# An expert's rows turned by matmuls with its 0/1 matrix, in place of a copy in memory, fetches and transposes

## The reference

```
logits = x @ w_router + b_router              # x: 288 x 1024, 32 experts
top_logit, top_e = top_k(logits, 4)
gate = softmax(top_logit)
for each expert e, over the rows that chose it:
    g, u = split(rows @ w_gu[e] + b_gu[e])     # 1024 -> 2 x 1024
    g = min(g, 7); u = clip(u, -7, 7)
    y = ((u + 1) * g * sigmoid(1.702 * g)) @ w_down[e] + b_down[e]
x = x + ga2 * (sum over a token's 4 experts of gate * y)
```

## Time and profile before

| what | value |
|---|---|
| median of three runs | 1684.99 us |
| profiled execution, own time | 1689.25 us |
| its span, first to last instruction | 1687.6 us |
| TensorE matmuls, busy | 1378.4 us, 82% |
| TensorE weight loads, busy | 724.2 us, 43% |
| VectorE, ScalarE, GpSimd, busy | 407.9, 287.8, 305.5 us |
| read from memory, written | 540.35 MB, 13.63 MB |
| mean rate | 324 GB/s |
| mean granted TensorE clock | 0.908 of full |

### The profile page before, as it was taken

How to read it: one execution, slowest core, us unless ns; L and a number is a source line. 1 busy time by engine, 2 the same in 40 slices (tenths; PEclk the granted TensorE clock), 3 DMA queues, 4 the chain that set the end, 5 groups by cost and what they waited for, 6 DMA issues and landing times.

```text
span 1687.6 us, 21658 instructions
## 1 busy us (share of the span) xinstructions
PE 1378.4 (82%) x8263; PEld 724.2 (43%) x8263; DVE 407.9 (24%) x775; ACT 287.8 (17%) x498; POOL 305.5 (18%) x289
## 2 busy tenths in 40 slices
PE   5697976787899768998989899898988989877763
PEld 2356753343589634343433434343343434322221
DVE  2256244534112442111111102111111111100006
ACT  1222443334143110100000101100010010000001
POOL 1345522231157110100101010100101010000003
PEclk9898997898899779999999999999999999986665
DMA  9663776696554738999999999999999999999963
GB/s 338 247 250 137 272 257 228 222 337 212 200 176 149 277 110 279 409 410 409 409 409 409 397 409 399 410 405 384 409 398 409 360 409 409 388 409 407 406 273 140
DMA packets 159403, 547.06 MB, mean 324 GB/s; under 512 B 14575, under 2 KB 14695, under 8 KB 155906
## 3 DMA queue, kind: packets, MB, share of 16 engines
q1 hardware_dynamic: 141856, 496.93, 76.7%
q0 software_dynamic: 16544, 45.72, 7.5%
q10 hardware_dynamic: 898, 3.01, 0.5%
HBM read 540.35 MB, written 13.63 MB: 328 GB/s over the span
## 4 chain that ended last, share of the span: by engine, by line
PE 50%; DMA 18%; SPq 17%; DVE 7%; ACT 4%; issue 3%; POOL 1%; ACTq 0%; POOLq 0%; DVEq 0%
PE PS L1488 44%; DMA wide<-in_w_gu 11%; SPq L505 9%; SPq L508 7%; PE PS L1655 4%; DMA ring<-in_w_in 3%; DMA wide<-in_w_down 2%; SPq L513 1%; DMA arena<-token_rows,rows_of 1%; ACT arena L969 1%; DMA arena<-in_x_sample 1%; PE PS L1818 1%; PE PS L1631 0%; DVE arena L1154 0%; DMA ring<-in_cache_mb_v 0%
## 5 line engine op out<-in xcount | busy, mean ns | idle before, releaser
L1488 PE MATMUL PS<-wide,arena 128*32 128x256 f32 (+2 forms) x4416 | 794.0, 509 | 93.4 <-DMA wide<-in_w_gu 55.8
L1488 PEld LDWEIGHTS PS<-wide,arena 128*32 128x32 f32 (+2 forms) x4416 | 322.9, 140 | 535.1 <-issue 328.9
L648 POOL DMA_INDIRECT choice_rows<-arena,rows_of x32 | 32.7, 1022 | 722.9 <-ACT arena L983 418.6
L582 POOL TENSOR_TENSOR WL<-ring,WL 128x1024 fp32r<-128x1024 f32 x48 | 117.9, 2467 | 147.7 <-ACT WL L725 147.6
L1488 PE MATMUL PS<-WH,WL 128*128 128x288 f32 x768 | 109.6, 305 | 13.5 <-issue 8.6
L1488 PEld LDWEIGHTS PS<-WH,WL 128*128 128x128 f32 x768 | 108.0, 197 | 17.3 <-issue 11.3
L969 ACT ACTIVATE arena<-PS 128x128 f32<-128x128 f32 (+2 forms) x64 | 24.5, 397 | 383.4 <-PE PS L1818 383.4
L725 ACT ACTIVATE WL<-ring 128x1024 fp32r<-128x1024 f32 x56 | 58.2, 1056 | 165.7 <-DMA ring<-in_w_in 97.0
L1386 DVE COPY small<-PS 128x1 f32<-128x1 f32 x32 | 5.1, 158 | 331.3 <-PE PS L1488 331.3
L1488 PE MATMUL PS<-WL,WH 128*128 128x512 f32 (+1 forms) x288 | 70.0, 402 | 17.1 <-DVE WH L1087 10.5
L1655 PE MATMUL PS<-cst,ring 128*128 128x128 f32 x512 | 65.6, 285 | 16.7 <-ACT arena L817 9.2
(11 more groups left out here) (271 smaller groups left out, 1102.0 us busy)
## 6 DMA issues: line engine op xcount, KB each, us to landing
wide<-in_w_gu SPq DMA_DIRECT2D x256, 1024.0 KB, 18.0
wide<-in_w_down SPq DMA_DIRECT2D x128, 1024.0 KB
ring<-in_w_ada SPq DMA_DIRECT2D x24, 1024.0 KB, 7.1
ring<-in_w_in SPq DMA_DIRECT2D x20, 1024.0 KB, 8.1
ring<-in_cache_sb_k SPq DMA_DIRECT2D x32, 256.0 KB, 4.8
ring<-in_cache_sb_k POOLq DMA_DIRECT2D x32, 256.0 KB, 5.6
ring<-in_cache_sb_v SPq DMA_DIRECT2D x32, 256.0 KB, 3.7
ring<-in_cache_sb_v POOLq DMA_DIRECT2D x32, 256.0 KB, 4.7
```

The lines of the kernel that those rows point to most:

```text
L582: pool.tensor_tensor(low, raw_half(h), high.bitcast(F32), ALU.subtract).then_inc(mix_low, 1)
L648: pool.indirect_dma_start(Y4.rearrange("t (h n) -> (t h) n", h=n), bass.IndirectOffsetOnAxis(ap=rows_of[:, at, 0:1], axis=0), yb[:, 0:D // ...
L1488: return T.matmul(out, lhsT, rhs, start=start, stop=stop, skip_group_check=True)
```

## The change

The tokens are no longer written to memory, and no rows are fetched. TensorE makes an expert's turned rows itself: for each of the 8 pieces of 128 features, three matmuls over the three tiles of tokens (128, 128 and 32), the stationary operand a piece of `h2n`, the moving one the expert's 0/1 matrix, 32, 64 or 128 columns wide. The sums land in PSUM banks 6 and 7 where the transposes left them. Since a 0/1 matrix is now needed until the turn is done, there are two, used in turn, and `place` waits for the turn of two experts before. GpSimd's first memset and the waits for fetches go.

```diff
-        XR = acc[:, 0, :]
+        onehots = [onehot, c3(acc[:, 0, 0:NT * P], P)]
+
+        def hot(it):
+            return onehots[it % 2 if isinstance(it, int) else 0]
...
-        H2 = nc.dram_tensor("token_rows", (NTOK, D), F32, kind="Internal").ap()
...
-            def fetch_rows(it, at, n):
-
-                if not isinstance(it, int) or it:
-                    pool.wait_ge(rows_turned, it)
-                pool.wait_ge(info_ready, it + 1)
-                pool.sem_inc(pool_step, 1)
-                pool.indirect_dma_start(
-                    XR[:, 0:D // n], None, H2.rearrange("t (h n) -> (t h) n", h=n),
-                    bass.IndirectOffsetOnAxis(ap=rows_of[:, at, 1:2], axis=0),
-                    bounds_check=NTOK * n - 1, oob_is_err=False).then_inc(rows_in, 16)
...
-            pool.wait_ge(h2_out, 32)
-            chain(pool.memset(XR, 0.0))
             n_big = 0
             for it in range(-1, NE):
-                if it + 1 < NE:
-                    fetch_rows(it + 1, (it + 1) % 3, WAYS[it + 1])
-                    if WAYS[it + 1] == 1:
-                        biases(it + 1, n_big)
-                        n_big += 1
+                if it + 1 < NE and WAYS[it + 1] == 1:
+                    biases(it + 1, n_big)
+                    n_big += 1
                 if it >= 0:
                     store_rows(it, it % 3, WAYS[it])
...
-            act.dma_start(H2[0:NPR, :].rearrange("(a p) n -> p a n", p=P), h2n[:, 0:2, :]).then_inc(h2_out, 16)
-            act.dma_start(H2[NPR:NTOK, :], h2n[0:NSM, 2, :]).then_inc(h2_out, 16)
...
-            def place(col, n):
-
+            def place(it, col, n):
+                if not isinstance(it, int):
+                    dve.wait_ge(rows_turned, it)
+                elif it > 1:
+                    dve.wait_ge(rows_turned, it - 1)
...
             def turn_rows(it, n):
-                pe.wait_ge(rows_in, (it + 1) * 16)
-                for k in range(DT // n):
-                    last = T.transpose(PS[:, 6 + k // 4, (k % 4) * P:(k % 4 + 1) * P], XR[:, k * P:(k + 1) * P], ident)
+                w, per = CAP // n, DT // n
+                for k in range(DT):
+                    at = k % per * P + k // per * w
+                    for i, (a, m) in enumerate(TILES):
+                        last = mm(PS[:, 6 + at // 512, at % 512:at % 512 + w], h2n[0:m, i, k * P:(k + 1) * P],
+                                  hot(it)[0:m, i, 0:w], i == 0, i == NT - 1)
                 last.then_inc(rows_turned, 1)
```

More of the change, by code:

```diff
@@ L325, in build @@
         oh_ready, info_fill, info_ready = sem("oh_ready"), sem("info_fill"), sem("info_ready")
-        late_pass, cnt_fill, ids_ready, h2_out, rows_in = sem("late_pass"), sem("cnt_fill"), sem("ids_ready"), sem("h2_out"), sem("rows_in")
+        late_pass, cnt_fill, ids_ready = sem("late_pass"), sem("cnt_fill"), sem("ids_ready")
         chunks_used = sem("chunks_used")
@@ L669, in _ @@
                         it = tp * LATE + r
-                        fetch_rows(it, 0, 1)
                         biases(it, it - FEW)
@@ L1366, in expert_ids @@
                 dve.sem_inc(ids_ready, 1)
-            def place(col, n):
+            def place(it, col, n):
[3 more added lines that the diff above has]
+                    dve.wait_ge(rows_turned, it - 1)
                 for i, (a, m) in enumerate(TILES):
                     if n > 1:
-                        last = TS(c3(onehot[0:m, i, :], CAP // n), iota[0:m, 0:CAP // n].unsqueeze(1).to_broadcast([m, n, CAP // n]),
+                        last = TS(c3(hot(it)[0:m, i, :], CAP // n), iota[0:m, 0:CAP // n].unsqueeze(1).to_broadcast([m, n, CAP // n]),
                                   pos[0:m, i, col:col + 1], None, ALU.is_equal)
@@ L1375, in place @@
                         one = slice(col, col + 1) if isinstance(col, int) else bass.ds(col, 1)
-                        last = TS(onehot[0:m, i, :], iota[0:m, :], pos[0:m, i, one], None, ALU.is_equal)
+                        last = TS(hot(it)[0:m, i, :], iota[0:m, :], pos[0:m, i, one], None, ALU.is_equal)
                 last.then_inc(oh_ready, 1)
@@ L1429, in few_dve @@
                     STT(hb[:, part], u[:, part], 1.0, g[:, part], ALU.add, ALU.mult).then_inc(hb_ready, 1)
-            place(RANKS[0], WAYS[0])
+            place(0, RANKS[0], WAYS[0])
             gates()
@@ L1434, in _ @@
             info(0, 0, WAYS[0])
-            place(RANKS[1], WAYS[1])
+            place(1, RANKS[1], WAYS[1])
             expert_ids()
@@ L1440, in _ @@
                 if it + 2 < NE:
-                    place(RANKS[it + 2], WAYS[it + 2])
+                    place(it + 2, RANKS[it + 2], WAYS[it + 2])
                 if WAYS[it] > 1:
@@ L1459, in _ @@
                         it = tp * LATE + r
-                        place(r, 1)
+                        place(it, r, 1)
                         info(it, 0, 1)
@@ L1808, in gather_info @@
                 for i, (a, m) in enumerate(TILES):
-                    last = mm(PS[:, 3, 0:3], onehot[0:m, i, :], val[0:m, i, one, :].rearrange("p a c -> p (a c)"),
+                    last = mm(PS[:, 3, 0:3], hot(it)[0:m, i, :], val[0:m, i, one, :].rearrange("p a c -> p (a c)"),
                               i == 0, i == NT - 1)
@@ L1921, in _ @@
                         turn_rows(it, 1)
+                        pe.wait_ge(info_ready, it + 1)
                         pe.wait_ge(xt_ready, it + 1)
```

## The result

The changed kernel takes 1847.36 us (median of four runs, 1844.56 to 1854.3) against 1685.17 of the kernel before (four runs): ratio 1.0968, 95% interval 1.0932 to 1.1004, slower by 157 to 169 us. The forecast was 1815 us, in a range of 1730 to 1860. Its profiled execution took 1844.56 us, with a span of 1842.9.

The account below looks back on a forecast made before the run. DMA weight loads bound the expert stage before; TensorE would after. Rounds +79, start +5, end -20 and clock falls +65 make +129 us on the profiled 1689.25, which lay 4 over the median: 1815 us, range 1730 to 1860.

Parts of the forecast that it names:

- its own case: Whole kernel: TensorE ends the rounds and its clock falls in the tiny and small experts' turns; 1815 us, chance 0.58.
- falls in all three turns: Rival on TensorE's clock: it falls in the big expert's turn too, +32 us, 1846 us; chance 0.08.
- The bound moves to TensorE: Expert stage: TensorE's work, 105.45 us a round at full clock, exceeds DMA's 96.1; a round near 112 us expected.
- The price of a turn at full clock: TensorE making an expert's turned rows: 48 pairs at 0.11 us plus row changes; 6.9 tiny, 7.3 small, 8.2 us big.
- The rival without a price for rows: TensorE's turns: row changes cost nothing, 5.3 us a turn, round 99.0; 1691 us at full clock, 1756 otherwise; chance 0.07.
- The step of the earlier trace: Count matmuls before the change: going to 32 rows takes 0.21 us against 0.11; the step back taken as equally dear.
- The clock: TensorE's clock halves inside the tiny and small experts' turns: 3.6 us a fall, two a round, +65 us over nine rounds.
- Fetches: Row fetches and token write on DMA: removing them wins at most 1.3 us per DMA-bound round.
- Start and end: First weights near 622 us, start +5 us; the last five tiny experts, their loads begun earlier, -20 us.
- The sum: Whole kernel: +64 us at full clock and +65 us for clock falls make +129 us on the profiled 1689.25 us.

## Why the prediction was right, and where it was off

**The time** lies in the range, but past the 1780 to 1840 us that the forecast gave for its own case, and it is the figure of a rival: falls in all three turns, 1846 us. There were three falls in some rounds, but the third isn't that rival's. The big expert's turn takes 8.51 us at a clock of 1.00 in each of the eight rounds that have one. So the rival's agreement is chance, and it is the rows that decide for the forecast's mechanism.

**The bound moves to TensorE**: right. No waits for weights inside the rounds, 332 GB/s (forecast under 370), a round of 116.2 us (forecast near 112).

**The price of a turn at full clock**: right. 8.44 us for the big expert's (forecast 8.2), which ran at 2.4 GHz throughout. The kernel with 128 columns tests the sum: the forecast's 105.45 us with 8.2 for all three turns is 107.65, measured 109.71, and of the 2.1 that are left the three turns at 8.4 make 0.6, and a fall behind the small expert's bias the rest (first matmuls 15.33 from start to start, for 13.9 at full clock). The rival without a price for rows gave 5.3 a turn and a round of 99.0; with 128 rows throughout, the turn is 5.36 (842.12 to 847.48) and the round 98.96. So the split of a turn into pairs at 0.11 and changes of rows was sound. The step of the earlier trace rows comes at each change: in the tiny expert's turn, at 1.00, it is 0.21 to the 32 rows (878.08 to 878.29) and 0.20 back (878.42 to 878.62). With 128 columns the turn takes 8.44 us against 5.36, with 48 pairs each: 0.19 more for each of sixteen changes, where the forecast had 0.10 and 0.08 for the stream waited for. The Trainium skill, TensorEngine Tiling, Key Properties, says that a change of tiling mode drains the engine. The trace agrees, by the 0.19 us that a change takes.

**The clock**: right in place, mis-sized. The forecast let it fall in the tiny and the small expert's turn, not in the big one's, and so it was. But it took 3.6 us for each fall, 7.2 a round, where the nine rounds show 116.16 - 105.45 = 10.7 on average. This is the term that is off. In the round shown: the fall in the tiny expert's turn costs 2.3 us in the turn (9.16 for 6.9), 0.5 in the hidden transposes and their copy, and 1.7 in the second matmuls (8.84 for 7.13), 4.5 in all; the one in the small expert's turn 2.2 in the turn, 0.25 behind it and 2.3 in the second matmuls (5.97 for 3.66), 4.7. The third fall had not been counted: it costs 0.4 in the small expert's bias matmuls and 2.9 in its first matmuls (16.89 for 13.95), 3.3 in this round. The three make 12.5, as 117.92 - 105.45 does; this takes the full-clock turns of 6.9 and 7.3 from the forecast, and no run here shows those two alone. Over the nine rounds the third fall, which five of them have, makes 1.3 us a round and the big expert's turn 0.2 over its 8.2; so about 2 of the 3.5 that were missing lie in the two falls that were foreseen. The forecast took the length of a fall from the earlier trace rows, 1.7 us for a stretch of 3.4 and as much again; in the round shown the falls in turns lasted 10.2 us. Why they last as long stays open: with zeroed rows the tiny expert's lasted 6.8 us in the round shown, yet in two of the nine rounds (turns at 1157.30 and 1467.70) it cost 1.6 us more, and with the third tile last, by an estimate from the 5.71 us of its small expert's turn, it cost about 4.5 us in eight of nine rounds, as in the changed kernel.

**Fetches**: worth little, as forecast, but under-sized. The forecast had 1.3 us a round, 12 in all, as all that a round can win without them; the kernel without them has rounds of 94.97, 2.4 less than before, and wins 22 us in all. This didn't touch the forecast time, as the weights no longer end the rounds.

**Start and end**: near in time, the start partly by luck. First weights came at 619.50 (forecast 622) after a first turn of 15 us at 1.2 GHz. But the stage was reached 3.1 us earlier than before (gather at 600.44 for 603.52), which no term had; in the other kernels of this document that gather starts anywhere from 594.37 to 603.14. And the clock was not up when the weights began, as the forecast had it for a gain of 1.5 us: the gather before them took 1.53 us, 0.92 at a full clock, and the clock was 0.50 up to 620.30. The last five experts were 21.5 us shorter (forecast 20).

**The sum**: forecast +129, measured in the spans +155. Rounds 176.3 in place of 79 + 65 = 144, 32 more (nine times 10.7 - 7.2); start, end and what follows 6 less than forecast. The falls are over by 32; less those 6, that makes the 26 that were missing.

By ratios the 163 us split so: changes of rows, with the clock that they cost, 108 (1.0968 to 1.0327); narrow columns 39 (to 1.0095); 48 weight loads a turn at full clock 38 (to 0.9867); less the 22 of the fetches. Taken the other way round, columns first, the columns make 51 (to 1.0668) and the changes 96 (to 1.0095), since both have a part in the falls. Of the 38, swapping the operands saves 26.

## What to carry to other kernels

Of two operands, the one with few columns belongs on the stationary side: what a matmul by a narrow matrix costs is its weight loads, here 48 of 128 columns in at least 5.3 us a turn, where 12 or 24 with the sides swapped took 1.6 to 5.6 (and 0.4 to 1.1 for the transposes), with no fall of the clock in a turn. The Trainium skill, TensorEngine Tiling, When to Use Tiling, advises this swap for moving sides of up to 64 columns. The runs agree, 1671.81 for 1847.36 us. For the big expert's 128 columns the swap itself saves nothing over padded rows: 5.61 us and 1.09 for the transposes, against 5.36. And where a tile is short of rows, filling it with zeros is cheaper than changing the rows from matmul to matmul: 1735.27 for 1847.36 us.

## What the runs showed of the chip that was not expected

The drains of changed rows weigh on the clock as well. The first turn at the start of the stage (48 pairs, 128 columns) stayed at 1.2 GHz for all of its 15.06 us with sixteen changes of rows; with two it took 7.45 us, and with none 7.24, back at 2.4 GHz within 4 us. The small expert's turns (64 columns) show the same later on: with sixteen changes the clock falls inside them, with two it falls behind them, with none it stays up.

The third fall is no steady one. In the round shown it lasts 6.8 us at 0.50 from 933.20 on, while TensorE is busy all the time. By the small expert's first matmuls five of nine rounds have it in the changed kernel, seven of nine with zeroed rows and seven of nine with 128 columns, and none with the third tile last. So neither the one-row bias matmuls before it, which are the same in all of them, nor the drains decide alone; what does stays open.
